# A selection penalty computed on two engines in a streaming encoder, with GpSimd doing six of its nine instructions

## The reference

```python
def _dsa_attend(q, k, v, iq, ik, iw, cid_q, cid_k, k_top):
    sc = jnp.einsum('bqhd,bkd->bqhk', iq, ik).astype(jnp.float32)
    score = jnp.einsum('bqhk,bqh->bqk', jax.nn.relu(sc), iw.astype(jnp.float32)) * IDX_SCALE
    adm = cid_k[None, :] <= cid_q[:, None]
    score = jnp.where(adm[None], score, -jnp.inf)
    kk = min(k_top, k.shape[1])
    _, sel = lax.top_k(score, kk)
    ...
    s = jnp.einsum('bqhd,bqsd->bqhs', q, k_sel).astype(jnp.float32) * (HD_C ** -0.5)
    s = jnp.where(valid[:, :, None, :], s, -jnp.inf)
    p = jax.nn.softmax(s, axis=-1).astype(v.dtype)
    return jnp.einsum('bqhs,bqsd->bqhd', p, v_sel)
```

## Time and profile before

| | |
|---|---|
| median of 3 runs | 2138.87 us (2136.68 to 2142.58) |
| the profiled execution, its time | 2146.08 us |
| its span from first to last instruction | 2144.4 us |
| busy in the span | PE 1932.9 us (90%), DVE 1392.8 us (65%), ACT 736.3 us (34%), POOL 259.0 us (12%) |
| penalty and search on DVE, their largest group | line 1759, 496 counts, 461.3 us |

### The profile page before, as it was taken

How to read it: one execution, slowest core, us unless ns; L and a number is a source line. 1 busy time by engine, 2 the same in 40 slices (tenths; PEclk the granted TensorE clock), 3 DMA queues, 4 the chain that set the end, 5 groups by cost and what they waited for, 6 DMA issues and landing times. The chain is left out here.

```text
span 2144.4 us, 27310 instructions
## 1 busy us (share of the span) xinstructions
PE 1932.9 (90%) x9670; PEld 1083.1 (51%) x9690; DVE 1392.8 (65%) x2961; ACT 736.3 (34%) x1678; POOL 259.0 (12%) x360
## 2 busy tenths in 40 slices
PE   3999999989999788999959999999899988889997
PEld 2634457555545555654444344565554455565443
DVE  3268488998796776533233684989897956665322
ACT  3353134233212544443243512334331134444332
POOL 0000132342100000001100002233221000000011
PEclk9999999999999999999979999999999999999998
DMA  8201214121323003223351022221205130022242
GB/s 281 99 25 67 79 47 136 61 81 50 113 73 77 18 6 94 89 67 132 128 193 55 25 71 74 92 97 60 96 30 153 38 72 13 26 76 87 95 149 103
DMA packets 151272, 178.34 MB, mean 83 GB/s; under 512 B 71408, under 2 KB 106736, under 8 KB 150864
## 3 DMA queue, kind: packets, MB, share of 16 engines
q1 hardware_dynamic: 123072, 139.19, 20.7%
q10 hardware_dynamic: 28064, 37.38, 4.9%
HBM read 119.72 MB, written 66.69 MB: 87 GB/s over the span
## 5 line engine op out<-in xcount | busy, mean ns | idle before, releaser
L914 PE MATMUL ps<-wring,xnT_arena 128*128 128x512 f32 (+2 forms) x2304 | 921.3, 542 | 0.0
L914 PEld LDWEIGHTS ps<-wring,xnT_arena 128*128 128x128 f32 x2304 | 405.0, 192 | 354.5 <-issue 337.7
L1759 DVE TENSOR_SCALAR_CACHE_REDUCE arena<-arena,theta 32x1056 bf16<-32x1056 f32 x496 | 461.3, 979 | 2.3
L1396 ACT COPY arena<-ps 128x512 f32<-128x512 f32 (+3 forms) x144 | 75.3, 523 | 449.4 <-PE ps L914 415.8
L1274 PE MATMUL ps<-wring,xnT_arena 128*128 128x512 f32 x512 | 223.9, 595 | 0.0
L2043 DVE TENSOR_REDUCE mneg<-ps 128x1 f32<-128x192 f32 (+9 forms) x148 | 113.9, 770 | 87.1 <-PE ps L1206 84.7
L1274 PEld LDWEIGHTS ps<-wring,xnT_arena 128*128 128x128 f32 x512 | 96.4, 191 | 115.4 <-issue 115.4
L1050 PEld LDWEIGHTS ps<-arena 128*128 128x128 f32 x488 | 69.6, 193 | 106.8 <-DVE arena L1866 78.2
L2206 POOL TENSOR_TENSOR arena<-arena 128x1024 f32<-128x1024 f32 (+1 forms) x16 | 35.5, 2216 | 727.2 <-DVE arena L1984 539.1
L1050 PE MATMUL ps<-arena 128*128 128x128 f32 x488 | 80.2, 287 | 39.5 <-DVE arena L1866 39.3
L1361 ACT COPY xnT_arena<-ps 128x512 f32<-128x512 f32 (+3 forms) x84 | 39.0, 464 | 188.9 <-PE ps L1218 141.6
(11 more groups left out here) (270 smaller groups left out, 2495.1 us busy)
## 6 DMA issues: line engine op xcount, KB each, us to landing
projected<-arena ACTq DMA_DIRECT2D x130, 256.0 KB, 2.0
arena<-residual SPq DMA_DIRECT2D x34, 512.0 KB, 5.2
wring<-in_w_in SPq DMA_DIRECT2D x16, 1024.0 KB, 7.6
o_bc<-projected SPq DMA_DIRECT2D x36, 384.0 KB, 3.7
wring<-in_w_in SPq DMA_DIRECT2D x6, 2048.0 KB, 8.8
wring<-in_w_out SPq DMA_DIRECT2D x8, 1024.0 KB, 5.5
residual<-arena SPq DMA_DIRECT2D x16, 512.0 KB, 2.6
out<-arena SPq DMA_DIRECT2D x16, 512.0 KB, 4.0
```

Source lines behind the costliest of these rows:

```text
L914: o = mm(bank(pbank(k), 0, w_), xnT[:, c, t * P:(t + 1) * P], w, start=(c == 0), stop=(c == CH - 1))
L1396: nc.scalar.copy(stage[s][:, 0:wide], bank(pbank(k), 0, wide)).then_inc(p_ev, 1)
L1759: V.tensor_scalar(cmp_out[0][r, (i % 2) * WMAX:(i % 2) * WMAX + uw[u]], score[u][r], th_, 0.0, op, ALU.add, accum_out=into[r, i:i + 1]).th ...
```

## The change

Two things are changed. First, six of the nine instructions of a unit's penalty go to POOL: sign, equal, rank test (split into a comparison and a product), sum and penalty. DVE keeps the count, the small subtraction and the scan. `PEN_STEPS` is 2 instead of 6. Five new semaphores hand over in both directions: DVE's first step waits for POOL's sign (`s_sign`), its second for POOL's comparison (`s_equal`); POOL waits for DVE's count and scan (`s_kept`, `s_rank`) before it goes on, and starts the next unit only when it has written the penalty before it. Second, `steps_by` is made anew: the 20 steps of the search get the share 3 times the jobs' (so they end at a third), the 16 penalty steps run from a share of 0.3 to 1, and a unit's latest job is eight jobs before its first DSA job.

```diff
-                    SEARCH, PEN_STEPS = len(UNITS) + 2, 6
+                    SEARCH, PEN_STEPS = len(UNITS) + 2, 2
...
-                            V.tensor_tensor(thr8, prefix.bitcast(F32), sg8, ALU.mult).then_inc(dve_own, one_more(own))
-                            dve.wait_ge(dve_own, own[0])
+                            V.tensor_tensor(thr8, prefix.bitcast(F32), sg8, ALU.mult).then_inc(s_found, 1)
+                            dve.wait_ge(s_found, 1)
...
                             if what == 0:
-                                V.tensor_scalar(score[u][r], score[u][r], sg8[r, i:i + 1], None, ALU.mult).then_inc(dve_own, one_more(own))
-                            elif what == 1:
+                                dve.wait_ge(s_sign, pen_at[u])
                                 V.tensor_scalar(keep, score[u][r], thr8[r, i:i + 1], 0.0, ALU.is_gt, ALU.add, accum_out=gcnt8[r, i:i + 1]).then_inc(dve_own, one_more(own))
-                                V.tensor_scalar(equal, score[u][r], thr8[r, i:i + 1], None, ALU.is_equal).then_inc(dve_own, one_more(own))
-                            elif what == 2:
-                                V.tensor_scalar(gcnt8[r, i:i + 1], gcnt8[r, i:i + 1], -1.0, float(TOP), ALU.mult, ALU.add).then_inc(dve_own, one_more(own))
-                                V.tensor_tensor_scan(rank, CB("oneb")[r].broadcast_to([r.stop, w]), equal, 0.0, ALU.mult, ALU.add).then_inc(dve_own, one_more(own))
-                            elif what == 3:
-                                V.scalar_tensor_tensor(out=equal, in0=rank, scalar=gcnt8[r, i:i + 1], in1=equal, op0=ALU.is_le, op1=ALU.mult).then_inc(dve_own, one_more(own))
-                            elif what == 4:
-                                V.tensor_tensor(keep, keep, equal, ALU.add).then_inc(dve_own, one_more(own))
+                                dve.wait_ge(dve_own, own[0])
+                                V.tensor_scalar(gcnt8[r, i:i + 1], gcnt8[r, i:i + 1], -1.0, float(TOP), ALU.mult, ALU.add).then_inc(s_kept, 1)
                             else:
-                                V.tensor_scalar(pen[u][r], keep, 0.0, -BIG, ALU.is_equal, ALU.mult).then_inc(pen_done, 1)
-                                dve.wait_ge(pen_done, pen_done_at[u])
+                                dve.wait_ge(s_equal, pen_at[u])
+                                V.tensor_tensor_scan(rank, CB("oneb")[r].broadcast_to([r.stop, w]), equal, 0.0, ALU.mult, ALU.add).then_inc(s_rank, 1)
...
-                    due = {job_no["dsa", u, 0] - 4: LATE + PEN_STEPS * (i + 1) for i, u in enumerate(PEN_ORDER)}
+                    due = {job_no["dsa", u, 0] - 8: LATE + PEN_STEPS * (i + 1) for i, u in enumerate(PEN_ORDER)}
...
-                        steps_by.append(min(total, max([int(total * share)] + [d for i, d in due.items() if i <= n])))
+                        steps_by.append(min(total, max([min(LATE, int(LATE * share * 3)) + int((total - LATE) * max(0.0, share - 0.3) / 0.7)] + [d for i, d in due.items() if i <= n])))
...
+                    pool.wait_ge(s_found, 1)
+                    for u in PEN_ORDER:
...
+                        if u != PEN_ORDER[0]:
+                            pool.wait_ge(pen_done, pen_at[u] - 1)
+                        G.tensor_scalar(score[u][r], score[u][r], sg8[r, i:i + 1], None, ALU.mult).then_inc(s_sign, 1)
+                        pool.wait_ge(s_sign, pen_at[u])
+                        G.tensor_scalar(equal, score[u][r], thr8[r, i:i + 1], None, ALU.is_equal).then_inc(s_equal, 1)
+                        pool.wait_ge(s_rank, pen_at[u])
+                        pool.wait_ge(s_kept, pen_at[u])
+                        G.tensor_scalar(rank, rank, gcnt8[r, i:i + 1], None, ALU.is_le).then_inc(pool_own, one_more(own))
...
+                        G.tensor_tensor(equal, rank, equal, ALU.mult).then_inc(pool_own, one_more(own))
...
+                        G.tensor_tensor(keep, keep, equal, ALU.add).then_inc(pool_own, one_more(own))
...
+                        G.tensor_scalar(pen[u][r], keep, 0.0, -BIG, ALU.is_equal, ALU.mult).then_inc(pen_done, 1)
```

More of the change, by code:

```diff
@@ L436, in encoder @@
         pen_done, pen_done_at = sem("pen_done"), steps(PEN_ORDER)
+        s_found, s_sign, s_equal, s_kept, s_rank = (sem(n) for n in ("s_found", "s_sign", "s_equal", "s_kept", "s_rank"))
+        pen_at = steps(PEN_ORDER)
         lf_min, lf_ln, lf_ready, lf_sums, lf_negc = (sem(n) for n in ("lf_min", "lf_ln", "lf_ready", "lf_sums", "lf_negc"))
@@ L1902, in _ @@
                     search(31 * SEARCH - LATE - at_search[0])
+                    at_pen = [0]
                     keep_equal = arena[:, stage_at:stage_at + WMAX].bitcast(BF16)
                     ranks = arena[:, stage_at + WMAX:stage_at + 2 * WMAX]
-                    at_pen = [0]
                     def late_search(n):
@@ L2200, in _ @@
                     pool.wait_ge(ka_ready, ka_ready_at[FKS[-1]])
+                    keep_equal = arena[:, stage_at:stage_at + WMAX].bitcast(BF16)
+                    ranks = arena[:, stage_at + WMAX:stage_at + 2 * WMAX]
+                    pool.wait_ge(s_found, 1)
+                    for u in PEN_ORDER:
+                        i = UNITS.index(u)
+                        r, w = slice(0, NS if u == "s" else P), uw[u]
+                        keep, equal, rank = keep_equal[r, 0:w], keep_equal[r, WMAX:WMAX + w], ranks[r, 0:w]
+                        if u != PEN_ORDER[0]:
[6 more added lines that the diff above has]
+                        G.tensor_scalar(rank, rank, gcnt8[r, i:i + 1], None, ALU.is_le).then_inc(pool_own, one_more(own))
+                        pool.wait_ge(pool_own, own[0])
+                        G.tensor_tensor(equal, rank, equal, ALU.mult).then_inc(pool_own, one_more(own))
+                        pool.wait_ge(pool_own, own[0])
+                        G.tensor_tensor(keep, keep, equal, ALU.add).then_inc(pool_own, one_more(own))
+                        pool.wait_ge(pool_own, own[0])
+                        G.tensor_scalar(pen[u][r], keep, 0.0, -BIG, ALU.is_equal, ALU.mult).then_inc(pen_done, 1)
                     for t in range(NT - 1):
```

## The result

The changed kernel takes 2167.61 us (median, 2166.97 to 2170.16), the kernel before in the same comparison 2138.28. The ratio is 1.0136, with a 95% interval of 1.0121 to 1.0151. The prediction of 2130 us was wrong in sign, and the time lies some 16 us above its range (2118 to 2152). Ratios here are of fast executions; two slow ones, 2185.3 us of the kernel before and 3339.51 us of the aligned kernel further down, are in none of them.

The account below looks back on a forecast made before the run. PE was taken as nearest to a bound, DVE's load counting only where PE or ACT waits. Gains and losses by place sum to 6.5 us a layer; two thirds, 4.3, over two layers from 2138.87 give 2130 us, range 2118 to 2152.

Parts of the forecast that it names:

- POOL's price of one-input work: POOL's one-input penalty instructions were priced at 0.30 + 0.84 w us, for w thousand keys.
- The bound from above: Upper price for POOL's one-input work: the same as two-input work, making all six instructions 85 us a layer, not 58.1.
- The first rival: POOL's chain is the bound, with waits at units 4, 5 and 3: 2146 us, at twice the price 2166; chance 0.22.
- (a): Jobs 22 to 27, second layer: DVE's count of unit s waits 1.5 us for POOL; job 26's reduce comes 1.8 us earlier.
- (b): Jobs 28 to 30: DVE waits 2.1 us at unit 4's count for POOL's 8.6 us chain; 1.1 us of gain left.
- (f): Jobs 51 to 55: DVE waits 1 us for POOL at unit 3, with two steps in one slot; loss of 0.8 us.
- (c): Jobs 31 to 36: POOL's chains of 5.9 and 6.7 us about fit the gaps; gain of 1.1 us.
- (d): Jobs 40 to 43, unit 2: PE's waits of 0.53 us for DVE and 1.40 us for ACT go; gain 1.9 us.
- (e): Job 47, unit 7: count and equal no longer stand before the reduce; gain of about 1 us.
- (g): Jobs 58 to 61, unit 8: PE's largest idle, 2.58 us, goes, less 0.3 us for the scan's new place; gain 2.2 us.
- Contention: Rival: POOL and DVE hold each other up, making POOL's chains 1.35 times as long: 2141 us; chance 0.06.
- The gain off the path: Rival: DVE is lighter but PE then waits for ACT and itself, so 2 us gained in all: 2137 us; chance 0.17.

Follow-up runs that it names:

- aligned kernel: Changed kernel with DVE's counts and scans moved to the jobs where POOL is ready and the search ending at job 22, POOL's instructions untouched: 2130.88 us, ratio 0.9962.
- run at the predicted price: Changed kernel with POOL's widths cut so each instruction costs what the prediction gave it, mask left out: 2130.42 us, ratio 0.9963.
- sign early: Changed kernel with the next unit's sign made on POOL ahead of its wait for the scan, not behind the penalty: 2162.67 us, ratio 1.0108.
- cut run: Changed kernel with all six POOL instructions of a unit cut to 32 columns, mask left out, handshakes and places kept: 2128.92 us, ratio 0.9949.
- the tail alone: Kernel before with only the last two penalty steps, sum and penalty, moved from DVE to POOL: 2139.76 us, ratio 1.0007.

## Why the prediction was wrong, step by step

**The step that failed is POOL's price of one-input work**, "0.30 + 0.84 w". It was read from fills (525 and 957 ns) and from a lone multiply of 4 elements, in which the element's own cost can't be seen. At 1088 keys that is 1.2 us; measured were 3.0 us for sign, equal and rank test and 3.9 for the penalty, 2.5 and 3.2 times as much. So the chain from s's scan to unit 4's sign is 13.2 us and not 8.6, and DVE waits 18.4 us a layer and not 4.6. The bound from above failed too: it assumed that one input costs no more than two, and the two-input instructions take 2.26 us at this width. These were sized well (2.5 us predicted). A rule of the Trainium skill pointed the same wrong way: "GPSIMD Engine Reference", section 4.1, has one-input work on GpSimd at about line rate. Here that holds for copies and multiply-add pairs, 0.83 ns an element, and for none of the four one-input forms of this change.

**The weight of a wait failed too.** The prediction counted two thirds of every wait and gain, because PE's direct waits on DVE were only 8.5 us a layer. With the waits as measured, 13.8 us a layer more than the 4.6, this gives 2130 + 2 x 13.8 x 2/3 = 2148 us, inside the range; the price alone doesn't explain the 2167.6. From the run at the predicted price (2.9 us of waits a layer) to the changed kernel 15.5 us more of waits a layer cost (1.0136 - 0.9963) x 2138 / 2 = 18.5 us a layer, a weight of 1.2 (1.0 to 1.4 by the intervals). The stretch from the first reduce of attention to the last shows where it goes. The second layer of the changed kernel, the one at the predicted price and the aligned one:

```profile
1751.12:2014.12 263.00, 222.13 (x1577) 149.87 (x1587) 136.06 (x277) 113.49 (x289) 99.58 (x49) 0.94 0.17 47
```
```profile
1731.40:1971.82 240.42, 209.22 (x1577) 141.45 (x1585) 135.79 (x277) 113.47 (x289) 55.62 (x49) 0.99 0.19 51
```
```profile
1734.36:1974.42 240.06, 211.20 (x1587) 142.88 (x1587) 135.86 (x277) 114.04 (x289) 99.56 (x49) 0.99 0.19 51
```

In both layers together the stretch is 522.6 us, against 480.2 and 480.7, and PE is busy in it for 439.4 us, against 418.2 and 423.6, with the same matmuls (a few of their records are missing from the traces). So of some 42 us lost in these executions 16 to 21 are longer matmuls, at a granted clock of 0.94 against 0.99 in the second layer. That is a term that the sum didn't have; the rest is PE's idle time.

The first rival had this mechanism and these places. Its waits came out nearly right, 12 us more than 4.6, or 16.6 a layer. In part that is luck. Its factor of 1.5 is that of all six instructions (85 to 58.1 us), but of the five in a chain two are two-input ones anyway: by its own bound the chain from s to 4 is 4 x 2.4 + 1.4 + 0.6 = 11.7 us, 1.36 times 8.6. The measured chain is 1.53 times, since one-input work was dearer than the bound. At 1.5 times the rival gave 2146 us, by the same two thirds.

The rival had 22 in 100, since the price that it needs was held to be unlikely: "decides from 1.3 times my price" is borne out as far as the runs go, at a price of 2.5 to 3.2 times.

**What leaves DVE** was right. The five groups of 49.4 us are gone and the groups that stay are what they were to within 0.6 us each. The page's 44.8 us are less; by the sums given with it, some 5 us of what left had overlapped with other instructions of DVE.

**The places and their waits** were right in place and wrong in size, for the price. (a) DVE waits 3.25 us, not 1.5, since the sign takes 2.95 and not 1.19. (b) The chain is 13.2 us, not 8.6, and the wait 6.47, not 2.1. (f) 4.60, not 1, and 0.7 more at the scan. With the predicted prices 2.9 us a layer are left, and the time is 2130 us: there the total held, though its waits of 4.6 did not. (c) had 1.1 us of gain between jobs 31 and 36, and units 5 and 6 wait 1.57 and 0.72 us there; 0.6 us are gained from job 29 to job 37.

**(d), (e), (g), the gains**, were seen where they were expected. Against the kernel before, the reduces of the changed one gain 1.9 us between jobs 37 and 47 of the second layer (2.9 expected) and 2.1 us between 56 and 60 (2.2 expected), and PE's idle of 2.58 us is gone. They drown in the 10 us lost by job 29 and the 6 us at job 54.

**The search's new spread** was one of the edits that "cost nothing". With DVE's own six steps the new places cost 12 us in all, and how much of that is the search's the runs don't tell. With a light DVE and a cheap POOL it isn't seen. The last penalty's lateness cost nothing, as expected: from the last reduce of attention to the end it is 154.1 us, and 154.9 before.

**The other rivals.** Contention is ruled out as the cause by the aligned kernel, with the same POOL work and 37 us less, and by the count's 983 to 987 ns. It does exist: the scan of 1.98 us beside POOL's sign, in "sign early", is 1.8 times its usual. The gain off the path is ruled out for the whole of DVE's 45 us by the cut run, though it is what the 12 us of the tail alone showed.

## What to carry over

A price on GpSimd has to come from a row with the same operations, not from another one-input instruction: among the forms tried here the number of inputs said little, and the operation or pair of operations decided. Where a second engine gets part of a chain, first work out when its result is ready and put the reader there; here the same instructions were 1.4% slower or 0.4% faster by the places of DVE's steps. And an engine that works in order holds back, while it waits, all that stands behind. So DVE's waits cost about their full length from the aligned kernel to the changed one, though DVE was idle for a third of the time.

## What the hardware showed that was not expected

- On GpSimd a multiply followed by an add of 0 takes 540 ns at 128x416, the multiply alone 1254 ns. Cheap were mult-add, mult-mult and add-mult (0.83 ns an element), also with a per-row scalar (612 ns) and in bf16; lone operations cost 2.5 ns, pairs with a comparison or a subtract 3.3 ns. A two-input multiply by a broadcast column (882 ns) is cheaper than the lone multiply by a scalar.
- bf16 in or out changes nothing on GpSimd: 1256 and 1254 ns for the lone multiply, 2242 and 2256 ns for sum and product at 1088.
- Behind a stall of 4.09 us PE's matmuls took 265 ns instead of 130, at a granted clock of 0.50 in those 2 us and 0.66 in the 10 us around.
- DVE's scan of 128x448 took 1.98 us beside a POOL instruction of 3.04 us that had started 0.13 us before it, and 1.09 us alone, in both layers; POOL's took no longer. A scan that started beside the last 0.7 us of another sign kept its time (1.35 us).
